# Retention's normalisation by pairs of heads, and the second pair's turn inside the output projection

## What is computed

```
def retention(x, w_in, w_out):              # 4 heads, 256 (q, k) and 512 (v, g) wide
    q, k, v, g = split(x @ w_in)
    ...                                     # rotary, decayed scores, o = scores @ v
    o = o * rsqrt(mean(o * o, axis=-1) + eps)        # per head of 512
    y = silu(g) * o.reshape(256, 4 * 512)
    return y @ w_out                        # 2048 -> 1024
```

## Time and profile before

| | us |
|---|---|
| median of 3 runs | 2842.05 (2841.74 to 2843.18) |
| the profiled execution | 2846.76 |
| its span, first to last instruction | 2845.0 |

### The profile page before, as it was taken

How to read it: one execution, slowest core, us unless ns; L and a number is a source line. 1 busy time by engine, 2 the same in 40 slices (tenths; PEclk the granted TensorE clock), 3 DMA queues, 4 the chain that set the end, 5 groups by cost and what they waited for, 6 DMA issues and landing times.

```text
span 2845.0 us, 38945 instructions
## 1 busy us (share of the span) xinstructions
PE 2681.7 (94%) x12618; PEld 2198.6 (77%) x12618; DVE 1766.0 (62%) x2439; ACT 1446.9 (51%) x2041; POOL 59.3 (2%) x85
## 2 busy tenths in 40 slices
PE   8987999998899979999999989999999999999998
PEld 6866787777777757788887878788778887778886
DVE  5645988856788866656455655554564655665554
ACT  4544776645566755544444425444544544554543
POOL 0000000000000000000000000000000000000000
PEclk9998999999899989999999989999999999999999
DMA  7544988944588974345553305455444654443653
GB/s 245 179 155 156 348 317 318 344 134 141 206 316 314 344 253 156 123 152 181 193 179 126 119 29 183 159 190 193 155 163 140 215 178 143 161 141 121 212 188 107
DMA packets 149961, 546.03 MB, mean 192 GB/s; under 512 B 17031, under 2 KB 17232, under 8 KB 149720
## 3 DMA queue, kind: packets, MB, share of 16 engines
q1 hardware_dynamic: 144664, 526.04, 53.7%
q0 software_dynamic: 4912, 17.43, 2.0%
q10 hardware_dynamic: 272, 1.05, 0.1%
HBM read 543.39 MB, written 2.63 MB: 192 GB/s over the span
## 4 chain that ended last, share of the span: by engine, by line
PE 82%; DVE 9%; ACT 3%; issue 3%; DMA 1%; POOL 1%; DVEq 0%; POOLq 0%; ACTq 0%; SPq 0%
PE bank L1688 24%; PE bank L1690 23%; PE bank L1689 23%; DVE low_w L905 3%; PE bank L1766 2%; PE bank L1884 1%; PE bank L2135 1%; PE bank L1897 1%; DVE low_d L911 1%; PE bank L2181 1%; PE bank L2197 1%; ACT tmp L741 1%; DVE y L957 1%; PE bank L2105 1%; POOL stat L446 1%
## 5 line engine op out<-in xcount | busy, mean ns | idle before, releaser
L905 DVE TENSOR_TENSOR low_w<-stage_w,high_w 128x1024 fp32r<-128x1024 f32 x784 | 944.2, 1221 | 404.8 <-ACT high_w L536 377.7
L1688 PE MATMUL bank<-high_w,xh 128*128 128x512 f32 x2624 | 1055.0, 402 | 34.1 <-DVE xl L918 10.1
L1690 PE MATMUL bank<-high_w,xl 128*128 128x512 f32 x2624 | 1030.6, 393 | 0.0
L1689 PE MATMUL bank<-low_w,xh 128*128 128x512 f32 x2624 | 1029.9, 392 | 0.0
L536 ACT ACTIVATE high_w<-stage_w 128x1024 fp32r<-128x1024 f32 x784 | 822.2, 1059 | 238.8 <-PE bank L1690 217.6
L1688 PEld LDWEIGHTS bank<-high_w,xh 128*128 128x128 f32 x2624 | 497.6, 190 | 153.7 <-issue 39.0
L1690 PEld LDWEIGHTS bank<-high_w,xl 128*128 128x128 f32 x2624 | 497.5, 190 | 107.0
L1689 PEld LDWEIGHTS bank<-low_w,xh 128*128 128x128 f32 x2624 | 498.6, 190 | 98.0 <-issue 0.5
L911 DVE TENSOR_TENSOR low_d<-stage_d,high_d 128x1024 fp32r<-128x1024 f32 x216 | 255.5, 1222 | 46.7 <-ACT high_d L543 46.7
L1688 PE MATMUL bank<-high_d,hidden_h 128*128 128x512 f32 x576 | 224.8, 390 | 2.8 <-DVE low_d L911 2.8
L1690 PE MATMUL bank<-high_d,hidden_l 128*128 128x512 f32 x576 | 224.4, 390 | 0.0
(11 more groups left out here) (256 smaller groups left out, 1884.6 us busy)
## 6 DMA issues: line engine op xcount, KB each, us to landing
stage_w<-in_wide SPq DMA_DIRECT2D x784, 512.0 KB, 4.6
stage_d<-in_down SPq DMA_DIRECT2D x216, 512.0 KB, 4.6
gain<-in_gains POOLq DMA_DIRECT2D x19, 512.0 KB, 4.8
skew<-bias_dram POOLq DMA_DIRECT2D x1, 1536.0 KB, 14.3
h<-in_x SPq DMA_DIRECT2D x2, 512.0 KB, 4.2
proj<-in_hg_consts POOLq DMA_DIRECT2D x1, 1024.0 KB, 7.3
proj<-skew POOLq DMA_DIRECT2D x1, 1024.0 KB, 9.8
tmp<-in_mem POOLq DMA_DIRECT2D x1, 1024.0 KB, 7.3
```

The source lines that it names most:

```text
L905: vec.tensor_tensor(low_w[:, w], stage_w[:, w], high_w[:, w].bitcast(F32), ALU.subtract)\
L1688: pe.matmul(o, hi, wh, start=start, stop=False)
L1689: pe.matmul(o, hi, wl, start=False, stop=False)
L1690: return pe.matmul(o, lo, wh, start=False, stop=stop)
```

## The change

The norm is split in two. For each pair of heads VectorE waits for four `ret_taken`, GpSimd takes a root of 4 columns, VectorE scales four tiles, and then it forms the low parts of that pair's turn before it comes to the next pair. `table_free` is signalled in the second pass. TensorE does the first turn, waits with `wait_kept` until it is kept, and hands the second turn to `pending`, so that it is done in block 0 ahead of rows 1. Block 1 has a wait of its own for the second turn. The number of products, transposes, scalings, copies and low parts is the same; a mean and a root are added, each half as wide.

```
@@ gpsimd
                 elif s.kind == "retention":
-                    root(16, T * RET_HEADS)
+                    for m in range(2):
+                        root(16 + T * RET_HEADS // 2 * m, T * RET_HEADS // 2)
                     after_retention(s)
@@ vector: retention
-                dve.wait_ge(ret_taken, 2 * RET_HEADS)
-                signal(table_free)
-                rstd(16, 8, RET_V)
                 o = pv(6144)
-                for j in range(RET_HEADS):
-                    for t in range(T):
-                        oj = o[:, t, j * RET_V:(j + 1) * RET_V]
-                        ins = vec.scalar_tensor_tensor(
-                            out=oj, in0=oj, scalar=stat[:, 16 + 2 * j + t:17 + 2 * j + t],
-                            in1=o[:, t, 4096 + j * RET_V:4096 + (j + 1) * RET_V], op0=ALU.mult, op1=ALU.mult)
-                    if j % 2:
-                        ins.then_inc(mixed, 1)
-                keep_split(s.turn, 0)
-                keep_split(s.turn + 1, 8)
+                for m in range(2):
+                    dve.wait_ge(ret_taken, 2 * RET_HEADS // 2 * (m + 1))
+                    if m:
+                        signal(table_free)
+                    rstd(16 + 4 * m, 4, RET_V)
+                    for j in range(2 * m, 2 * m + 2):
+                        for t in range(T):
+                            oj = o[:, t, j * RET_V:(j + 1) * RET_V]
+                            ins = vec.scalar_tensor_tensor(
+                                out=oj, in0=oj, scalar=stat[:, 16 + 2 * j + t:17 + 2 * j + t],
+                                in1=o[:, t, 4096 + j * RET_V:4096 + (j + 1) * RET_V], op0=ALU.mult, op1=ALU.mult)
+                    ins.then_inc(mixed, 1)
+                    keep_split(s.turn + m, KC * m)
@@ tensor: residual
+                        if not half and k == 1:
+                            wait_kept(PLAN[PLAN.index(s) - 1].turn + 1)
@@ tensor: retention
-                for m in range(2):
+                def turn_heads(m):
                     for t in range(T):
                         turn(s.turn + m, v[:, :, m * D:(m + 1) * D], t, (mixed, m + 1))
+
+                turn_heads(0)
+                wait_kept(s.turn)
+                pending[1, 0] = lambda: turn_heads(1)
```

## The result

| | before | changed |
|---|---|---|
| median, 20 runs each, us | 2841.59 (2836.55 to 2845.00) | 2835.95 (2828.31 to 2839.19) |
| span of the profiled execution | 2845.0 | 2835.1 |
| idle ahead of the first turn | 6.01 | 0 |
| first turn, second turn, us of TensorE | 3.67, 3.65 | 1.91, 1.91 |
| idle behind the first turn | 1.50 | 2.57 |

The ratio is 0.9979, with a 95% interval from 0.9973 to 0.9986: 5.6 us less by the medians, 4.0 to 7.7 by the interval. The forecast was 7.0 less and faster by over 0.2%; the median lies just short of that bound (0.198%). The interval shows that there is a gain and leaves open whether it is over 0.2%. The spans of the two profiled executions differ by 9.9, which is more than the stage gave: single executions of one kernel lie up to 11 us apart here (2828.31 to 2839.19).

What follows compares the result with a forecast made beforehand. TensorE (82% of the chain) bounds it, with idle time in the retention stage. Projection 10.08 earlier, less 1.75 for the turn, plus 0.4 clock, gives 8.7; less 1.7 for a clock fall, 7.0: 2842.05 to 2835.0 us, range 2831.6 to 2838.6.

Steps and rivals of the forecast that it cites:

- What bounds: Retention stage: one path where TensorE stands still; what is taken out ahead of the blocks reaches the end.
- First half of the norm: VectorE and GpSimd, under the last products: root 1.04, scaled by 169.1, so TensorE's 6.17 us wait goes whole.
- First turn and the new wait: TensorE before the projection: turn 1.91 instead of 3.67 at full clock, then idle grows from 1.50 to 2.65 us.
- Second half: Norm of the second pair, behind VectorE's low parts: done at 178.5, asked for at 180.1, covered by 1.6 us.
- The turn in the block: Second turn, moved into block 0 of the projection: costs TensorE 1.75 us at full clock.
- The clock: TensorE behind the 2.65 us idle piece: 3.4 us at half clock, losing 1.7; bounds 0 and 5.1.
- Rival A: No clock fall behind the idle piece ahead of the projection: gain 8.7 us, 2833.3; chance 0.27.
- rival B: Long low clock stretch, 10.2 us at half clock, 5.1 lost: gain 3.6 us, 2838.5; chance 0.10.
- D: Slower: TensorE stays at half clock behind the gap ahead of the projection, 28.8 us for over 0.2%; chance 0.03.
- GpSimd's loads: Five loads behind the second turn meet block 2's weights: taken as 0 us, at worst 3.3 late.
- the sum of bytes: Block 2's weights: 4.2 MB at 332 GB/s takes 12.7 us, to 198.6; fourth piece wanted at 198.4, plus 1.6.
- rival C: `mixed` 1, `mixed` 2 or block 2's weights come late: gain 3.7 at worst, 2838.4; middle 2836.5; chance 0.13.

Runs made afterwards that it cites:

- both load experiments: Changed kernel with GpSimd's 1 MB skew load issued after the first mixture of experts, ratio to before 0.9974; changed kernel with a sixth 1 MB load, 0.9982.
- the changed kernel again: The changed kernel, unaltered, profiled and timed once more against the kernel before: ratio 0.9973, median 2834.64 us against 2841.93.
- The filler: Changed kernel plus 24 transposes that nothing reads, between the first turn and the wait for it: ratio to before 0.9972.
- each half: Changed kernel cut to one part: norm by pairs alone, ratio to before 0.9995; second turn inside block 0 alone, 1.0000.

## Why the prediction was right, point by point

**What bounds.** Right: the stage was one path, and what left it came out behind the projection, 6.1 in Y, and at the end, 5.6 (4.0 to 7.7) in time. The projection's first product is earlier by 15.50 - 5.34 = 10.16; 10.08 was forecast.

**First half of the norm.** Forecast: root of four columns 1.04, scaled by 169.1, TensorE not waiting. Measured: 1.04, 169.35 in a trace in which everything stands 0.37 later, and no idle.

**First turn and the new wait.** 1.91 and 2.65 of idle were forecast; 1.91 and 2.57 came. The row that proved the link, VectorE's last low part 0.1 before the product, isn't named by the profile, which says "issue".

**Second half.** 178.5 forecast, 178.71 - 0.37 = 178.3 measured. The cover held and was 3.3, not 1.6 (178.71 to 182.03), since the slow clock put off the moment at which TensorE asks; the forecast's date for it had no fall in it. The turn in the block cost 1.66 (182.03 to 183.69), with a first product behind it that is 0.08 longer; 1.75 was forecast.

**The clock.** The forecast took the fall, 3.4 us long. It came in this profile and in each of the three others that kept this idle piece of 2.57 (both load experiments and the changed kernel again). The filler put its price at 1.8, the term said 1.7. Rival A is what the filler shows and didn't happen; rival B and D didn't either: the dense products brought the clock back as they had in the earlier trace rows. Part of this was luck. The forecast chose between two rows, one with a fall and one without, and its reasons for the choice (a longer piece, sparser products ahead) were not tested each by itself. Those two idle pieces, of 2.50 us, come back in all twelve profiles of this case: behind the one between 256 and 269 us the clock fell in one of twelve, behind the one between 724 and 737 in five of twelve (mean 0.56 to 0.58 in the 3.5 us behind it). So the length of an idle piece alone doesn't say whether the clock falls, and what else decides stays open.

**The term that was mis-sized: GpSimd's loads.** I took 0, with 3.3 at worst; it is 1.0. Up to block 2 the changed kernel was 7.1 ahead, as forecast; behind it 6.1. This is read from VectorE's first addition to `h`, which waits for block 1's rows 0; before:

```profile
201.64 0.69 DVE L1028 TENSOR_TENSOR h<-h,bank 128x512 f32<-128x512 f32 x1 [3.12 <-PE bank L1690]
```

and changed, 6.74 earlier in a trace in which the last head stands 0.37 later:

```profile
194.90 0.69 DVE L1029 TENSOR_TENSOR h<-h,bank 128x512 f32<-128x512 f32 x1 [3.12 <-PE bank L1691]
```

The step that failed is the landing time of the stage pieces, which I took from the earlier trace rows, and not the sum of bytes. I checked by the sum that the fourth piece would be in time, and took 0 because landings of 3.1 to 5.5 were on record, from the old order, where only the tail of one load ran beside. The parts of the sum held: 2.1 MB of GpSimd's were to be left, at 332 GB/s. In the changed kernel 3.12 MB moved from 187.9 to 197.3, which is 332 GB/s, and by queue (packets, MB, share; q0 is GpSimd's, q1 SyncE's):

```profile
q0 software_dynamic: 451, 2.10, 68.1%
q1 hardware_dynamic: 272, 1.03, 27.9%
```

But all four pieces took 9.3 to 10.3 to land. ScalarE's copy of the second came 2.1 later than where it stands without the skew load (199.70, against 197.06 in a trace in which the last head stands 0.50 earlier), more than the 1.6 that I had given VectorE ahead of TensorE. TensorE was held by the low part of the second piece (the product at 202.07 starts 0.80 behind the one before it, where 0.23 is usual) and a little by that of the fourth (at 205.03, 0.31 behind). The fourth landed at 191.9 + 10.2 = 202.1, 1.5 later than the sum gives from the measured start (187.9 + 12.7 = 200.6).

The Trainium skill's rule (DMA: Bandwidth & Descriptors, Queues, rings and completion order), that a DMA engine takes turns between its queues, agrees in part. The first piece landed at 197.2, 2.1 ahead of the skew load (186.7 + 12.6 = 199.3), so it didn't wait for all of it, and from 193 to 194 SyncE's queue moved 0.18 of 0.37 MB. But from 189 to 191 all 0.65 MB were GpSimd's, and SyncE's queue had moved 0.02 MB by 192, 4 us after its first piece was asked for; in the old order it had moved 0.13 MB 2 us after (asked for at 194.7, by 196.7). They began as GpSimd's load of constants, 1 MB, landed (185.7 + 6.7 = 192.4); whether that is the cause isn't shown. The skew load isn't: with it moved, SyncE's queue had moved no more than 0.04 MB by 192 either. So taking turns meant neither going first nor an even share from the start, and that was my mistake in using it. This was rival C's mechanism, at under a third of its worst price.

Forecast 7.0 less this 1.0 is 6.0; 6.1 was measured in Y, and 5.6 in time. The time's interval, 4.0 to 7.7, holds both 6.0 and 7.0: that the forecast was 1.0 too high is told by Y alone.

## What to carry to other kernels

Price a halved stage by the idle piece that is left, not by the work that moved: here each half gave 3.4 and 0.9 and the whole 6.1, since only the whole left an idle piece under 3 us, and what is left here still costs a fall of the clock. Ask of each wait which part of what it waits for is read next; splitting one wait was worth 3.2 to 3.5 us in Y, more than half of the change again. When work is brought forward and weights are asked for closer behind other transfers, date each piece that then shares the queues with its own due time; one sum of bytes for the last of them isn't enough, and neither are landing times from an order in which they didn't meet.

## What the runs showed of the hardware

An idle piece of 2.57 us on TensorE, behind the heads' products and a turn, was followed by 3.4 us at 1.2 GHz in four profiles of four, one of 0.93 or 0.94 in none of three. Pieces of 2.50 us between dense products, in two other places, were followed by a fall in 6 cases of 24. Useless transposes in the piece of 2.57 kept 2.4 GHz, for a gain of 1.8 us in Y. A load of 0.5 MB took 9.3 to 10.3 us to land when the first of four was asked for with some 2.1 MB of GpSimd's still to move, where it had taken 3.1 to 5.5, and 12.6 instead of 9.8 passed for the last of GpSimd's. GpSimd's root takes 1.02 to 1.04 us for four columns, between 0.56 for one and 1.68 for eight.
